# The attention tiles of a pair run from the last to the first, and the values leave PSUM as high and low part

## Chip, cores and metric

The kernel runs on one core of one Trainium2 chip. The metric is the device time of one execution in microseconds; a time is the median of the runs.

## What is computed

One layer of a streaming encoder, for a prompt of 512 frames and a sample of 32 frames with 512 cached ones. Only the part around the change, cut from the reference:

```
qkv = z[..., :3 * D_ATTN].reshape(B, T, 3, N_HEADS_A, HEAD_DIM_A)
q, k, v = qkv[:, :, 0], qkv[:, :, 1], qkv[:, :, 2]
s = einsum('bqhd,bkhd->bhqk', q, k) * (HEAD_DIM_A ** -0.5) + bias
o_a = einsum('bhqk,bkhd->bqhd', softmax(s), v)      # 8 heads x 64; a frame sees its 64-frame chunk
                                                    # and the 8 chunks before it, so all keys up to there
o_b, wkv1 = rwkv7_time_mix(zx, ...)                 # a gated delta rule over the same 8 heads x 64
merged = gates[..., :D_MODEL] * (o_a @ w_out_attn) + gates[..., D_MODEL:] * (o_b @ w_out_rwkv)
```

Before this stand a norm and the combined input projection, behind it the output projection, a residual and a SwiGLU network. All is float32. For the large products each operand is split into a high part that TensorE takes as fp32r and a low part (value minus high part), and three products are summed.

## The kernel before

The five engines run hand-written programs, each in its own order, and meet only at semaphores. The stage that the change touches lies between the input projection and the product with `w_out_attn`, from 347 to 560 us. It mixes two jobs.

The first job is the RWKV recurrence. The prompt is cut into 16 tiles n, four for each of the four head pairs hp, and two tiles a and b are worked on at once in one round of 16 slots. Slots 0 and 1 form the products of a tile (`p_scores`, masked by `v_masks` into XX, CTs and BDs), slot 2 `p_cv`, slots 3 to 12 five levels of a triangular inverse (a step `p_level_p` and a step `p_level_x` in turn, each followed by a small VectorE operation on Pb or XX), slot 13 `p_wu`, slots 14 and 15 `p_out`. There are 8 rounds, so 128 slots g; a head pair has 32 slots p, two rounds.

The second job, attention, is put into the same slots by hand. At the end of slot p each engine runs what is due for the head pair: scores of a tile at the slots `A_S`, the softmax in the slots behind, and the product with the values at the slots `A_PV`. A tile has 128 query frames of both heads e of the pair; prompt tile t has (t + 1) * 128 keys, and tile 4 is the sample with 512 cached keys and 32 own ones. For head e of a tile the order is: `v_scores` (VectorE, adds the bias and takes the maximum, slot S + e), `a_exp` (ScalarE, S + 1 + e), `v_scale` (VectorE: reciprocal and a multiplication in place in `s_sb`, S + 2 + e), `transposes` (TensorE, S + 3 + e), `a_turned_p` (ScalarE copies to `pt_sb`), `values` (TensorE), `a_values` (ScalarE). For the tile with 512 keys the last steps come one slot later. The next tile's `scores` wait for the semaphore `o_ev`, since both use PSUM banks 6 and 7. In `A_PV[0:2]` the sample's own scores are made (`own_scores`, `v_own`), in `A_PV[2]` the cached keys are transposed.

`a_values` copies a tile's values from PSUM into `oaT`, which is the space of the queries, `qk[:, 0:HP]`. In slot 31 of a pair ScalarE copies all 548 columns to `oah` (rounding to fp32r; it lies over the keys, `qk[:, HP:2 * HP]`), and in slot 0 of the next pair VectorE writes `oal`, the difference, over the queries.

GpSimd prepares the next pair's operands in `prelude` (eleven steps over 548 columns, from the start of a pair's first round on, for pairs 1 to 3 in the pair before), and the low parts of weight units, `low(i)`. ScalarE makes their high parts, `high(i)`; that of the first unit of `w_out_attn` is issued inside the slots:

```
                a_attn(g)
                if g == 16 * NR_ - 12:
                    act.wait_ge(sc_mm, NT - TT)
                    act.wait_ge(saved, HP - 1)
                    high(U_OA, U_OA % 2)
```

This is slot 20 of pair 3. `low(U_OA)` waits for it on GpSimd. After the last slot come the sample's recurrence (`p_scores(NT)` and on), the chain of states, and the product with `w_out_attn` (`attn_tile`), which reads `oah` and `oal`.

Of the kernel before, what the change touches and what calls it, by code (L numbers as in the profile page):

```python
# [17 lines left out]
F32 = mybir.dt.float32  # L18
# [32 lines left out]
def build(nc, x_prompt, x_sample, cache_k, cache_v, state_wkv, state_shift, c_prompt, c_sample, w_ada, b_ada,  # L51
# [34 lines left out]
    with ctx:  # L86
# [63 lines left out]
        oaT = qk[:, 0:HP]  # L150
# [192 lines left out]
        A_S = (0, 6, 12, 18, 25)  # L343
        A_PV = (5, 11, 17, 24, 30)

        def head_at(p, after, late=0):

            for t, s in enumerate(A_S):
                for e in range(2):
                    if p == s + after + e + (late if t == 3 else 0):  # L350
                        return t, e
            return None

        def scored(t):

            return TILES[t][1], (t + 1) * P if t < TT else T + TS
# [193 lines left out]
        def _(pool):  # L550
# [85 lines left out]
            link(pool.memset(E1[1][:, 0:1], 1.0))  # L636
            for hp in range(HP):
                if hp:
                    pool.wait_ge(sc_mm, (hp - 1) * TT)
                    pool.wait_ge(gm_dve, (hp - 1) * TT)  # L640
                    for k in range(11):
                        prelude(pool, link, hp, k)
                else:
                    pool.wait_ge(ew_done, 1)
                q = hp % 2
                for x, y in zip(four, (kt[q], bh[q], kh[q], rt[q], bl[q], kl[q])):
                    pool.tensor_copy(x[:, hp, :], y[:, S0:W])
                pool.tensor_copy(four[6][:, hp, :], zs[:, 2 * HP + hp, 1 + S0:1 + W])
                pool.tensor_copy(e4[:, hp:hp + 1], E1[q][:, W:W + 1]).then_inc(saved, 1)
# [13 lines left out]
        def _(act):  # L663
# [187 lines left out]
            def a_exp(hp, t, e):  # L851
                rows_, n = scored(t)
                act.wait_ge(s_biased, 2 * (hp * KS + t) + e + 1)
# [4 lines left out]
            def a_turned_p(hp, t, e):  # L858
                i = hp * KS + t
# [8 lines left out]
            def a_values(hp, t):  # L868
                c0, rows_ = TILES[t]
                act.wait_ge(o_mm, hp * KS + t + 1)  # L870
                act.activation(oaT[:, hp, c0:c0 + rows_], ps[:, 6, 0:rows_], ACT.Copy).then_inc(o_ev, 1)

            def a_attn(u):
# [12 lines left out]
                if p == 31:  # L886
                    act.wait_ge(o_ev, hp * KS + KS)
                    act.activation(oah[:, hp, :], oaT[:, hp, :], ACT.Copy).then_inc(oah_done, 1)
# [110 lines left out]
        def _(dve):  # L999
# [199 lines left out]
            def v_scores(hp, t, e):  # L1199
                rows_, n = scored(t)  # L1200
                i = hp * KS + t
# [21 lines left out]
            def v_scale(hp, t, e):  # L1223
                rows_, n = scored(t)
                i = 2 * (hp * KS + t) + e + 1
# [5 lines left out]

            def v_attn(u):
                hp, p = divmod(u, 32)
                if p == 0 and hp:
                    dve.wait_ge(oah_done, hp)
                    tt(oal[:, hp - 1, :], oaT[:, hp - 1, :], oah[:, hp - 1, :].bitcast(F32), ALU.subtract)  # L1236
                if hp == HP:
                    return
# [25 lines left out]
            v_attn(16 * NR_)  # L1264
# [172 lines left out]
        def _(pe):  # L1437
# [296 lines left out]
            def scores(hp, t):  # L1734
                c0, rows_ = TILES[t]
                i = hp * KS + t
                if i:
                    pe.wait_ge(o_ev, i)
                if t in (1, 2):
                    pe.wait_ge(own_ev, 2 * hp + t)  # L1740
                if t == 3:
# [12 lines left out]
            def transposes(hp, t, e):  # L1754
                rows_ = TILES[t][1]
                pe.wait_ge(p_scaled, 2 * (hp * KS + t) + e + 1)
# [7 lines left out]
            def values(hp, t):  # L1764
# [3 lines left out]
                pe.wait_ge(pt_ev, 2 * (hp * KS + t) + 2)  # L1768
# [74 lines left out]
            def chain(c):  # L1843
# [6 lines left out]
                ins.then_inc(chain_mm, 1)  # L1850
            p_scores(NT)
# [157 lines left out]
```

## Time and profile before

| What | Value |
|---|---|
| median of 3 runs | 1149.13 us (1146.98 to 1151.62) |
| the profiled execution | 1151.87 us, its span 1149.8 us |
| TensorE busy | 1080.1 us, 94% |
| VectorE, ScalarE, GpSimd busy | 400.1, 342.1, 362.5 us |
| TensorE's share of the chain that ended last | 85% |
| mean granted clock of TensorE | 0.967 of full speed |

The busy shares are means over stages of different kind. The rows further down are of the mixing stage only. A timeline row gives the start, the duration, engine, line and operation with the tile written and those read, and in brackets how long the engine had stood idle before and what ended that. PE is TensorE, DVE VectorE, ACT ScalarE, POOL GpSimd.

### The profile page before, as it was taken

The page shows a single profiled execution, that of the slowest core. Times are in us where ns is not written, and L with a number is a line of the kernel's source. Part 1 is how long each engine was busy: PE and PEld are TensorE (multiplying, and loading weights), DVE is VectorE, ACT ScalarE, POOL GpSimd, SP SyncE. Part 2 cuts the span into 40 slices and gives each one's busy share as a digit, 9 for nine tenths or more (in the row PEclk, how much of TensorE's full clock was granted, in tenths as well). Part 3 has the DMA queues.
Part 4 walks back from the last instruction along what each step waited for, and adds up shares of the span by engine and source line. Part 5 has one row for each costly group of instructions (what it writes and reads, how often), then busy time and mean ns, then how long its engine had stood idle before and what let it go on. Part 6 is the DMA issues. An engine that isn't in the chain of part 4 may idle for free.

```text
span 1149.8 us, 25415 instructions
## 1 busy us (share of the span) xinstructions
PE 1080.1 (94%) x11068; PEld 991.9 (86%) x11068; DVE 400.1 (35%) x928; ACT 342.1 (30%) x605; POOL 362.5 (32%) x246
## 2 busy tenths in 40 slices
PE   6799999999998988999897899999999999899995
PEld 5698899999896766777785799999999999899995
DVE  2400100085054666666436746322222222100003
ACT  4521122233333444445121223332232232211112
POOL 0554443333315041301120233334334334243330
PEclk9899999999998999999995999999999999999998
DMA  9865556233201000040250322222422322223211
GB/s 367 296 229 184 183 184 212 96 126 127 85 30 35 21 3 20 12 156 2 85 152 10 123 92 74 74 73 73 109 73 74 109 73 66 72 76 94 82 50 78
DMA packets 115882, 117.31 MB, mean 102 GB/s; under 512 B 5284, under 2 KB 102736, under 8 KB 112472
## 3 DMA queue, kind: packets, MB, share of 16 engines
q1 hardware_dynamic: 111296, 110.74, 30.0%
q10 hardware_dynamic: 4504, 5.36, 1.5%
q8 instruction: 67, 1.10, 0.4%
q14 instruction: 15, 0.12, 0.0%
HBM read 104.59 MB, written 11.49 MB: 101 GB/s over the span
## 4 chain that ended last, share of the span: by engine, by line
PE 85%; DVE 7%; DMA 2%; ACT 2%; issue 1%; SPq 1%; POOL 1%; DVEq 0%; ACTq 0%; POOLq 0%
PE ps L1439 82%; DMA ada_w<-in_w_ada 2%; PE ps L1758 2%; SPq L430 1%; DVE s_sb L1196 1%; POOL w_lo L567 1%; PE ps L1658 1%; DMA gring<-g_d 0%; DVE oal L1236 0%; DVE s_sb L1230 0%; PE ps L1978 0%; DVE Pb L1167 0%; DVE y_sb L1432 0%; DVE ss8b L1335 0%; ACT y_sq L992 0%
## 5 line engine op out<-in xcount | busy, mean ns | idle before, releaser
L567 POOL TENSOR_TENSOR w_lo<-w_raw,w_hi 128x2048 fp32r<-128x2048 f32 (+1 forms) x67 | 287.5, 4290 | 633.7 <-ACT w_hi L697 633.7
L1439 PE MATMUL ps<-hh,w_hi 128*128 128x274 f32 x1376 | 292.1, 294 | 5.0 <-DVE hl L1050 3.5
L1439 PE MATMUL ps<-hh,w_lo 128*128 128x274 f32 x1376 | 290.3, 292 | 0.0
L1439 PE MATMUL ps<-hl,w_hi 128*128 128x274 f32 x1376 | 288.4, 291 | 0.0
L1439 PEld LDWEIGHTS ps<-hh,w_hi 128*128 128x128 f32 x1376 | 220.3, 191 | 11.7 <-issue 9.5
L1439 PEld LDWEIGHTS ps<-hl,w_hi 128*128 128x128 f32 x1376 | 219.8, 191 | 0.0
L1439 PEld LDWEIGHTS ps<-hh,w_lo 128*128 128x128 f32 x1376 | 219.7, 191 | 0.0
L697 ACT ACTIVATE w_hi<-w_raw 128x2048 fp32r<-128x2048 f32 (+1 forms) x67 | 119.3, 1781 | 115.0 <-PE ps L1439 110.6
L1439 PE MATMUL ps<-ah,w_hi 128*128 128x274 f32 x352 | 74.1, 292 | 3.8 <-DVE al L1411 3.8
L1439 PE MATMUL ps<-ah,w_lo 128*128 128x274 f32 x352 | 74.1, 292 | 0.0
L1439 PE MATMUL ps<-al,w_hi 128*128 128x274 f32 x352 | 74.0, 292 | 0.0
L1439 PEld LDWEIGHTS ps<-ah,w_hi 128*128 128x128 f32 x352 | 56.5, 192 | 4.0 <-issue 4.0
L1439 PEld LDWEIGHTS ps<-ah,w_lo 128*128 128x128 f32 x352 | 56.4, 191 | 0.0
L1439 PEld LDWEIGHTS ps<-al,w_hi 128*128 128x128 f32 x352 | 56.4, 191 | 0.0
L1403 DVE TENSOR_TENSOR ff_a<-ps,rstd 128x548 f32<-128x548 f32 x22 | 16.0, 729 | 113.7 <-PE ps L1439 113.6
L978 ACT ACTIVATE ah<-ff_a 128x548 f32 (+1 forms) x22 | 14.6, 664 | 133.8 <-DVE ff_a L1407 133.8
L1370 DVE SCALAR_TENSOR_TENSOR xT<-ps,mod,xT 128x274 f32<-128x274 f32 (+1 forms) x16 | 8.0, 500 | 132.7 <-PE ps L1439 132.7
L1439 PE MATMUL ps<-XX,Pb 64*64 64x64 f32 x672 | 42.5, 230 | 2.6 <-DVE Pb L1167 2.6
L1439 PE MATMUL ps<-Pb,XX 64*64 64x64 f32 x536 | 38.2, 238 | 2.0 <-DVE Pb L1167 2.0
L1439 PEld LDWEIGHTS ps<-XX,ATs 64*64 64x64 f32 x672 | 26.8, 147 | 14.7 <-issue 9.0
L1439 PE MATMUL ps<-XX,ATs 64*64 64x64 f32 x672 | 34.3, 240 | 3.9 <-DVE XX L1177 2.0
L1439 PEld LDWEIGHTS ps<-Pb,XX 64*64 64x64 f32 x536 | 29.0, 146 | 9.4 <-DVE Pb L1167 7.0
(354 smaller groups left out, 1493.9 us busy)
## 6 DMA issues: line engine op xcount, KB each, us to landing
w_raw<-in_w_ffn_in SPq DMA_DIRECT2D x44, 512.0 KB, 4.5
w_raw<-in_w_in SPq DMA_DIRECT2D x42, 512.0 KB, 4.9
ada_l<-in_w_ada SPq DMA_DIRECT2D x16, 1024.0 KB, 6.0
ada_w<-in_w_ada SPq DMA_DIRECT2D x8, 1024.0 KB, 14.2
w_raw<-in_w_ffn_out SPq DMA_DIRECT2D x16, 384.0 KB, 3.9
w_raw<-in_w_ffn_out SPq DMA_DIRECT2D x16, 320.0 KB, 3.2
g_d<-gst SPq DMA_DIRECT2D x16, 274.0 KB, 2.6
gring<-g_d SPq DMA_DIRECT2D x16, 274.0 KB, 4.3
```

The source lines that it names most:

```text
L430: sp.dma_start(ada_w[k][:, :], ada_rows(0, k)).then_inc(ada_in[k], 16)
L567: pool.tensor_tensor(w_lo[:, s, 0:cols], w_raw[:, s, 0:cols], w_hi[:, s, 0:cols].bitcast(F32), ALU.subtract).then_inc(lo_done, 1)
L697: act.activation(w_hi[:, s, 0:cols], w_raw[:, s, 0:cols], ACT.Copy).then_inc(hi_done, 1)
L978: act.activation(ah[:, i - U_UP, :], ff_a[:, :], ACT.Copy).then_inc(ah_done, 1)
L1196: return dve.tensor_tensor_reduce(out=out, in0=x, in1=y, scale=-1.0, scalar=first, op0=ALU.add, op1=ALU.min, accum_out=low)
L1370: link(stt(xa[:, 0:H], ps[:, 2 * q, 0:H], g(0), xa[:, 0:H], ALU.mult, ALU.add))
L1403: tt(halves(ff_a[:, :]), pair(1), halves(rstd2[:, :]), ALU.mult).then_inc(pair_free, 1)
L1439: return pe.matmul(out, lhsT, rhs, start=start, stop=stop)
L1658: ins = pe.transpose(bank(q, 2)[:, i * P:(i + 1) * P], x, ident[:, :])
L1758: ins = pe.transpose(ps[:, 6 + e, b * rows_:(b + 1) * rows_], s_sb[0:rows_, e, b * P:(b + 1) * P], ident[0:rows_, 0:rows_])
```

## The change

The prompt tiles of a pair are taken in the order 3, 2, 1, 0, then the sample (`A_TILE`), and the slots are spaced anew: the tile with 512 keys has slots 0 to 6. The helpers are now called with the place i in this order, and look up the tile t. Since a key tile is no longer needed once the query tile of the same frames is done, `a_values` writes the fp32r high part of a tile straight from PSUM over its keys, and the new `v_values` on VectorE writes the low part, PSUM minus high part, over its queries; `o_ev` is now raised by VectorE. `oaT`, the whole-pair copy in slot 31 and the whole-pair subtraction in the next slot 0 are gone. GpSimd zeroes the four padding columns of both parts once, and TensorE waits for the last `o_ev` ahead of `p_scores(NT)`.

```diff
--- before.py
+++ after.py
@@ -147,7 +147,6 @@
         kc_raw, vcs = at("kc_raw", [P, TT, P], RAW + 2560), at("vcs", [P, TT, P], RAW + 4608)
         pt_sb, s_sb, rsum = at("pt_sb", [P, 2, T + P], HL + 7168), at("s_sb", [P, 2, T + TS], LO + 2560), \
             at("rsum", [P, 2, 4], LO + 6912)
-        oaT = qk[:, 0:HP]
         oah, oal = at("oah", [P, HP, W], E + 8768, F32R), at("oal", [P, HP, W], E, F32R)
 
 
@@ -340,19 +339,21 @@
             return [x[:, c] for x in (kt[q], bh[q], kh[q], rt[q], bl[q], kl[q])] + [zs[:, 2 * HP + hp, 1 + t * P:1 + (t + 1) * P]]
 
 
-        A_S = (0, 6, 12, 18, 25)
-        A_PV = (5, 11, 17, 24, 30)
+        A_S = (0, 7, 13, 19, 25)
+        A_PV = (6, 12, 18, 24, 30)
+        A_TILE = list(range(TT - 1, -1, -1)) + [TT]
 
         def head_at(p, after, late=0):
 
-            for t, s in enumerate(A_S):
+            for i, s in enumerate(A_S):
                 for e in range(2):
-                    if p == s + after + e + (late if t == 3 else 0):
-                        return t, e
+                    if p == s + after + e + (late if i == 0 else 0):
+                        return i, e
             return None
 
-        def scored(t):
-
+        def scored(i):
+
+            t = A_TILE[i]
             return TILES[t][1], (t + 1) * P if t < TT else T + TS
 
         def prelude(eng, link, hp, k):
@@ -634,6 +635,8 @@
                 low(i, i % 2)
             pool.wait_ge(unit_mm, U_OA)
             link(pool.memset(E1[1][:, 0:1], 1.0))
+            for x in (oah, oal):
+                link(pool.memset(x[:, :, T:S0].bitcast(F32), 0.0))
             for hp in range(HP):
                 if hp:
                     pool.wait_ge(sc_mm, (hp - 1) * TT)
@@ -848,15 +851,15 @@
                     i = act.activation(NN[:, hp, 2 * t + c, :], b[:, L:2 * L], ACT.Copy)
                 i.then_inc(gm_act, 1)
 
-            def a_exp(hp, t, e):
-                rows_, n = scored(t)
-                act.wait_ge(s_biased, 2 * (hp * KS + t) + e + 1)
+            def a_exp(hp, i, e):
+                rows_, n = scored(i)
+                act.wait_ge(s_biased, 2 * (hp * KS + i) + e + 1)
                 v = s_sb[0:rows_, e, 0:n]
                 act.activation(v, v, ACT.Exp, bias=rsum[0:rows_, e, 1:2], scale=-1.0, accum_out=rsum[0:rows_, e, 0:1])\
                    .then_inc(p_done, 1)
 
-            def a_turned_p(hp, t, e):
-                i = hp * KS + t
+            def a_turned_p(hp, i, e):
+                t, i = A_TILE[i], hp * KS + i
                 n = (t + 1) * P if t < TT else TT * TS
                 act.wait_ge(pt_mm, 2 * i + e + 1)
                 if i and e == 0:
@@ -865,10 +868,10 @@
                     act.activation(pt_sb[0:TS, e, n:n + TS], ps[0:TS, 6 + e, n:n + TS], ACT.Copy)
                 act.activation(pt_sb[:, e, 0:n], ps[:, 6 + e, 0:n], ACT.Copy).then_inc(pt_ev, 1)
 
-            def a_values(hp, t):
-                c0, rows_ = TILES[t]
-                act.wait_ge(o_mm, hp * KS + t + 1)
-                act.activation(oaT[:, hp, c0:c0 + rows_], ps[:, 6, 0:rows_], ACT.Copy).then_inc(o_ev, 1)
+            def a_values(hp, i):
+                c0, rows_ = TILES[A_TILE[i]]
+                act.wait_ge(o_mm, hp * KS + i + 1)
+                act.activation(oah[:, hp, c0:c0 + rows_], ps[:, 6, 0:rows_], ACT.Copy).then_inc(oah_done, 1)
 
             def a_attn(u):
                 hp, p = divmod(u, 32)
@@ -883,9 +886,6 @@
                 if p == A_PV[2]:
                     act.wait_ge(kct_mm, hp + 1)
                     act.activation(kcT[:, :], ps[:, 7, :], ACT.Copy).then_inc(kct_ev, 1)
-                if p == 31:
-                    act.wait_ge(o_ev, hp * KS + KS)
-                    act.activation(oah[:, hp, :], oaT[:, hp, :], ACT.Copy).then_inc(oah_done, 1)
 
             for g in range(16 * NR_):
                 rnd, p = divmod(g, 16)
@@ -1196,9 +1196,9 @@
                 return dve.tensor_tensor_reduce(out=out, in0=x, in1=y, scale=-1.0, scalar=first, op0=ALU.add, op1=ALU.min,
                                                 accum_out=low)
 
-            def v_scores(hp, t, e):
-                rows_, n = scored(t)
-                i = hp * KS + t
+            def v_scores(hp, i, e):
+                rows_, n = scored(i)
+                t, i = A_TILE[i], hp * KS + i
                 dve.wait_ge(s_mm, i + 1)
                 if i:
                     dve.wait_ge(pt_mm, 2 * i - 1 + e)
@@ -1220,22 +1220,25 @@
                 low_of(s_sb[0:TS, e, T:T + TS], ps[0:TS, 7, e * TS:(e + 1) * TS],
                        bias[0:TS, hp * 2 + e, T - P:T - P + TS], HUGE, rsum[0:TS, e, 3:4]).then_inc(own_ev, 1)
 
-            def v_scale(hp, t, e):
-                rows_, n = scored(t)
-                i = 2 * (hp * KS + t) + e + 1
+            def v_scale(hp, i, e):
+                rows_, n = scored(i)
+                i = 2 * (hp * KS + i) + e + 1
                 dve.wait_ge(p_done, i)
                 dve.reciprocal(rsum[0:rows_, e, 2:3], rsum[0:rows_, e, 0:1]).then_inc(rs_inv, 1)
                 dve.wait_ge(rs_inv, i)
                 v = s_sb[0:rows_, e, 0:n]
                 sts(v, v, rsum[0:rows_, e, 2:3], None, ALU.mult).then_inc(p_scaled, 1)
 
+            def v_values(hp, i):
+                c0, rows_ = TILES[A_TILE[i]]
+                c = slice(c0, c0 + rows_)
+                dve.wait_ge(oah_done, hp * KS + i + 1)
+                tt(oal[:, hp, c], ps[:, 6, 0:rows_], oah[:, hp, c].bitcast(F32), ALU.subtract).then_inc(o_ev, 1)
+
             def v_attn(u):
                 hp, p = divmod(u, 32)
-                if p == 0 and hp:
-                    dve.wait_ge(oah_done, hp)
-                    tt(oal[:, hp - 1, :], oaT[:, hp - 1, :], oah[:, hp - 1, :].bitcast(F32), ALU.subtract)
-                if hp == HP:
-                    return
+                if p in A_PV:
+                    v_values(hp, A_PV.index(p))
                 if head_at(p, 2, 1):
                     v_scale(hp, *head_at(p, 2, 1))
                 if head_at(p, 0):
@@ -1261,7 +1264,6 @@
                 if p == 9 and rnd % 2 and rnd < NR_ - 1:
                     v_bonus(rnd // 2 + 1)
                 v_attn(g)
-            v_attn(16 * NR_)
 
 
             dve.wait_ge(gm_act, NT)
@@ -1731,14 +1733,14 @@
                 p_chunks(q, part, (bank(q, 0)[:, L:2 * L], bank(q, 2)[:, L:2 * L]),
                          (bank(q, 1)[:, L:2 * L], bank(q, 2)[:, 3 * L:4 * L])).then_inc(gm_mm, 1)
 
-            def scores(hp, t):
+            def scores(hp, i):
+                t = A_TILE[i]
                 c0, rows_ = TILES[t]
-                i = hp * KS + t
-                if i:
-                    pe.wait_ge(o_ev, i)
-                if t in (1, 2):
-                    pe.wait_ge(own_ev, 2 * hp + t)
-                if t == 3:
+                if hp or i:
+                    pe.wait_ge(o_ev, hp * KS + i)
+                if i in (1, 2):
+                    pe.wait_ge(own_ev, 2 * hp + i)
+                if i == 3:
                     pe.wait_ge(kct_ev, hp + 1)
                 for e in range(2):
                     q_ = qk[part[e], hp, c0:c0 + rows_]
@@ -1751,9 +1753,10 @@
             def own_scores(hp, e):
                 mm(ps[0:TS, 7, e * TS:(e + 1) * TS], qk[part[e], hp, S0:W], qk[part[e], HP + hp, S0:W]).then_inc(own_mm, 1)
 
-            def transposes(hp, t, e):
+            def transposes(hp, i, e):
+                t = A_TILE[i]
                 rows_ = TILES[t][1]
-                pe.wait_ge(p_scaled, 2 * (hp * KS + t) + e + 1)
+                pe.wait_ge(p_scaled, 2 * (hp * KS + i) + e + 1)
                 for b in range(min(t + 1, TT)):
                     ins = pe.transpose(ps[:, 6 + e, b * rows_:(b + 1) * rows_], s_sb[0:rows_, e, b * P:(b + 1) * P],
                                        ident[0:rows_, 0:rows_])
@@ -1761,11 +1764,12 @@
                     ins = pe.transpose(ps[0:TS, 6 + e, TT * TS:(TT + 1) * TS], s_sb[0:TS, e, T:T + TS], ident[0:TS, 0:TS])
                 ins.then_inc(pt_mm, 1)
 
-            def values(hp, t):
+            def values(hp, i):
+                t = A_TILE[i]
                 rows_ = TILES[t][1]
                 c = [slice(hp * P + e * DH, hp * P + (e + 1) * DH) for e in range(2)]
                 o = [ps[part[e], 6, 0:rows_] for e in range(2)]
-                pe.wait_ge(pt_ev, 2 * (hp * KS + t) + 2)
+                pe.wait_ge(pt_ev, 2 * (hp * KS + i) + 2)
                 if t == TT:
                     pe.wait_ge(vc_in, hp * 16 + 16)
                 for b in range(min(t + 1, TT)):
@@ -1848,6 +1852,7 @@
                                  MT[part[e], a, c, :] if c < NCH else MT4[part[e], a, :],
                                  SS[part[e], c if c < NCH else NCH + 1, a, :])
                 ins.then_inc(chain_mm, 1)
+            pe.wait_ge(o_ev, HP * KS)
             p_scores(NT)
             pe.wait_ge(gm_dve, NT)
             pe.wait_ge(gm_act, NT)
```

## Rows read from the trace of the kernel before

**Rows 1.** Windows: pairs 0 and 1, and the sum over the stage.

```profile
core 0: us, PE busy (x) PEld busy (x) DVE busy (x) ACT busy (x) POOL busy (x), PEclk, DMA share, GB/s
347.20:399.60 52.40, 47.68 (x1006) 37.35 (x1010) 29.98 (x120) 22.37 (x73) 16.43 (x28) 0.90 0.09 26
399.60:449.70 50.10, 43.95 (x1018) 34.70 (x1011) 33.09 (x123) 22.24 (x77) 15.76 (x23) 0.97 0.05 14
...
sum 212.80, PE 189.09 PEld 149.75 DVE 132.79 ACT 92.11 POOL 53.83; mean PE 37.82 PEld 29.95 DVE 26.56 ACT 18.42 POOL 10.77
```

**Rows 2.** Waits of TensorE from 347 to 560 us.

```profile
engine line waited for: us in total, times, longest us
PE ps L1439 <- DVE BDs L1159: 9.5, 5, 3.1
PE ps L1439 <- DVE Pb L1167: 4.6, 11, 0.6
```

**Rows 3.** Timeline of VectorE, start of pair 1.

```profile
402.00 1.32 DVE L1162 TENSOR_TENSOR XX<-XX,dg 128x256 f32<-128x256 f32 x1
403.24 1.86 DVE L1236 TENSOR_TENSOR oal<-qk,oah 128x548 fp32r<-128x548 f32 x1
405.02 0.28 DVE L1196 CUSTOM_DVE_ANT_0 s_sb<-ps,bias 128x128 f32<-128x128 f32 x1
...
405.23 0.41 DVE L1156 TENSOR_TENSOR XX<-ps,nM 128x256 f32<-128x256 f32 x1
...
405.77 0.41 DVE L1159 TENSOR_TENSOR BDs<-ps,inclU 128x256 f32<-128x256 f32 x1
```

**Rows 4.** Timeline of GpSimd, start of pair 1.

```profile
401.67 1.37 POOL L374 TENSOR_TENSOR kh<-kh,zs 128x548 f32<-128x548 f32 x1
```

**Rows 5.** Timeline of TensorE: the waits at four places.

```profile
353.35 1.12 PE L1439 MATMUL ps<-XX,ATs 64*64 64x64 f32 x16 [1.49 <-ACT KC L834]
...
406.23 0.45 PE L1439 MATMUL ps<-tk,CTs 64*64 64x64 f32 x8 [3.13 <-DVE BDs L1159]
...
424.76 0.55 PE L1758 MATMUL ps<-ident,s_sb 128*128 128x128 f32 x3 [0.69 <-DVE s_sb L1230]
...
504.67 0.45 PE L1439 MATMUL ps<-tk,CTs 64*64 64x64 f32 x8 [1.09 <-DVE BDs L1159]
```

**Rows 6.** Timeline of TensorE: scores of 128 and 512 columns, one level step.

```profile
400.90 0.49 PE L1439 MATMUL ps<-qk 64*128 64x128 f32 x4
...
430.46 1.13 PE L1439 MATMUL ps<-qk 64*128 64x512 f32 x4 [0.17 <-ACT kcT L885]
431.52 0.68 PE L1439 MATMUL ps<-XX,ATs 64*64 64x64 f32 x16
```

**Rows 7.** Windows of TensorE alone, start of pair 2.

```profile
core 0: us, PE busy (x), PEclk, DMA share, GB/s
...
456.00:462.00 6.00, 5.67 (x76) 0.50 0.00 0
```

**Rows 8.** Groups by form on VectorE, and line L871 on ScalarE.

```profile
L1196 DVE CUSTOM_DVE_ANT_0 s_sb<-ps,bias 128x512 f32<-128x512 f32 x8 | 5.5, 687 | 7.5 <-PE ps L1439 7.5
...
L871 ACT ACTIVATE qk<-ps x20: 204/278/280, 358.9 to 546.4; 128x128 f32<-128x128 f32 x16, 128x32 f32<-128x32 f32 x4
```

**Rows 9.** Timelines of ScalarE, GpSimd and VectorE, pair 3, slots 20 to 22.

```profile
531.42 0.72 ACT L855 ACTIVATE s_sb<-s_sb,rsum 128x512 f32<-128x512 f32 x1 [0.19 <-DVE rsum L1196]
...
532.14 1.90 ACT L697 ACTIVATE w_hi<-w_raw 128x2048 fp32r<-128x2048 f32 x1
...
534.27 4.74 POOL L567 TENSOR_TENSOR w_lo<-w_raw,w_hi 128x2048 fp32r<-128x2048 f32 x1 [63.58 <-ACT w_hi L697]
...
534.15 0.48 DVE L1230 TENSOR_SCALAR s_sb<-s_sb,rsum 128x512 f32<-128x512 f32 x1
```

**Rows 10.** Line L1117 on VectorE.

```profile
engine op xcount: duration ns min/median/max, first and last start us, forms
L1117 DVE TENSOR_SCALAR kk<-zs,par x4: 491/493/4744, 263.5 to 269.0; 128x548 f32<-128x548 f32 x4
```

**Rows 11.** Timelines of VectorE and GpSimd, pair 1, slots 8 and 9.

```profile
415.82 0.79 DVE L1230 TENSOR_SCALAR s_sb<-s_sb,rsum 128x256 f32<-128x256 f32 x1
...
415.11 1.34 POOL L395 TENSOR_TENSOR kh<-kh,E 128x548 f32<-128x548 f32 x1
```

**Rows 12.** Timelines of VectorE and TensorE after the last slot.

```profile
548.75 0.73 DVE L1236 TENSOR_TENSOR oal<-qk,oah 128x548 fp32r<-128x548 f32 x1 [0.95 <-ACT oah L888]
...
549.74 0.68 PE L1439 MATMUL ps<-SS,MT 64*64 64x64 f32 x16 [0.74 <-DVE SS L1268]
```

## The prediction

> **What bounds the kernel.** I read the busy shares first (TensorE is busy 94% of the span), then the chain that ended last (85% TensorE), so only what makes TensorE wait or run slowly can move the end. All edits lie in the 128 slots of the mixing stage. The windows [rows 1] show TensorE at work for 47.7 of 52.4 us in pair 0, for 43.95 of 50.1 in pair 1, and for 189.1 of 212.8 in the stage, so it is idle some 24 us. The table of waits [rows 2] puts 9.5 of these on the masked products (BDs) and 4.6 on Pb. No edit here can give back more than that and its clock effects.
>
> The largest wait stands at the start of a pair [rows 3]: VectorE masks tile a, then takes 1.86 us for the low part of the pair before (oal), then masks tile b, and TensorE stands 3.13 us until BDs of tile b is there [rows 5]. Both VectorE operations are long because GpSimd holds something they need: its tensor operation runs from 401.67 to 403.04 [rows 4], and the addition to XX that starts at 402.00 ends 0.3 us after that [rows 3]. In the last pair GpSimd is idle and the same wait is 1.09 us. After its wait TensorE runs a while at half clock [rows 7].
>
> **Removed.** Four whole-pair oal operations on VectorE (slot 0 of the next pair, and one after the last slot) and four whole-pair oah copies on ScalarE. Between masks(a) and masks(b) 1.86 us of VectorE goes away in pairs 1 and 2.
>
> **Put in the same place.** The last tile is now the first in a pair, so scores of 512 columns stand in slot 0: TensorE 1.13 us for 0.49 [rows 6], +0.64, which is only moved work (it leaves slot 18), and VectorE 0.69 for 0.28 [rows 3, 8], +0.41, between masks(a) and masks(b). Pairs 1 and 2: masks(a) ends at about 403.3, scores to 404.0, BDs(b) 0.95 us later (405.23 to 406.18 in [rows 3]) at 404.9. TensorE has 0.64 more to do and is free at 403.75 instead of 403.1; it waits about 1.2 us for 3.13: -1.9 each. But the scale of these 512 columns by 1/sum (0.48 us free, [rows 9]) now falls in slots 3 and 4, where GpSimd begins a run of operations as long as that in [rows 4]; each of the two heads can be held up to one operation. I take 0.8 exposed per pair (between 0 and 2.7), so -1.1 each. Pair 3, GpSimd idle: 1.09 becomes about 0.3, -0.8. Pair 0 had no oal, so it only gets the longer work: ScalarE's exponential of 512 columns (0.72, [rows 9]) for one of 128 stands ahead of the KC copies for which TensorE waits 1.49 us [rows 5]: +0.5. Sum of the starts: -2.5 us (bounds -6 and +1).
>
> **The new hand-over.** Each of 20 tiles: ScalarE writes oah from PSUM (0.28, the operation it had, [rows 8]) and VectorE adds a subtraction from PSUM, 0.28 for 128 columns by the equally wide operation in [rows 3], 20 times 5.3 us in all against 5.2 removed. It reads PSUM and one SBUF tile, as the mask operation does that starts at 405.23. VectorE waits in its queue for the values (at the end of slot PV) and for ScalarE; behind it stand the slot's own scores and the next slot's Pb or XX. It is held about 0.65 us after the values' last product. TensorE meanwhile has the next slot's level step (0.6 to 1.0 us, [rows 6]) and waits for o_ev only behind that, and the scores then cover VectorE's lag: nothing for most. Where VectorE is already late I charge 0.2 us twice per pair (slots 8 to 10, and 25 where the sample's scores are due): +1.6 in four pairs. Without that cover each costs 0.65.
>
> **The middle of a pair.** The tile at slots 13 to 18 has 256 columns instead of 384, and its transposes move one slot later. The 0.69 us wait at 424.76 [rows 5] goes; but nothing then stands between p_out and the next p_scores, which must wait for both evacuations (about 0.4 to 0.5), and the second scale now stands behind masks(c) (0.2, and 0.2 again at masks(d)). I count +0.35 there and -0.38 where the first tile's two 0.69 us operations no longer delay Pb in slot 19: zero, give or take 0.3 per pair.
>
> **The end.** VectorE's chain of states waited for oah and for oal (0.73 us), and TensorE 0.74 us for it [rows 12]. Both are gone from there: -0.8. The new wait for o_ev ahead of the sample's p_scores was met a slot and a half earlier. Two small memsets on GpSimd come ahead of preparations that then wait for ScalarE anyway: nothing, at most 0.3 us.
>
> **The step that costs.** In pair 3 ScalarE issues high(U_OA) (1.90 us) at the end of slot 20, and GpSimd's subtraction of 2,048 columns follows 0.23 us after its end, for 4.74 us [rows 9]. Before, both exponentials of the tile in slot 18 came ahead of high, and the second scale began at 534.15, 0.12 us ahead of GpSimd. Now the tile starts in slot 19: its second exponential is in slot 21, behind high in ScalarE's queue. So the second scale, which needs it, cannot start before about 0.5 us (exponential and reciprocal, estimate) after GpSimd has begun. What a tensor_scalar with SBUF alone does then is seen from 263 us on, under the same subtraction of another unit: at least one of L1117's four takes 4.74 us, where the median is 0.49 [rows 10]. So VectorE stands for about 4 us; TensorE has one level step left, then waits for this scale to transpose: from about 4.85 us after slot 19's start to 8.8 us: +3.9. The first scale I place 0.4 us ahead of GpSimd; if it fails too, the stall is about 1 us longer. Bounds of the term: 0 and 5.5.
>
> The nearest rows for a scale itself are milder: a 256-column scale that starts at 415.82, inside GpSimd's operation of 1.34 us, takes 0.79 us and is done 0.16 us after that operation's end [rows 11]. Read as "held till GpSimd is done" this also gives the 4 us; read as "up to 0.4 us longer" it gives no stall and a sum 6 us lower, rival (a) below. I take the first, because the end of the scale follows GpSimd's end and because of L1117.
>
> The Trainium skill, page SBUF — State Buffer, section "Who interferes with whom", speaks against this change: the two engines share a port pair under an exclusive lock, tensor_scalar can enter the modes that take it, and whichever issues second "fully blocks" for the other's whole instruction. By that rule the stall is there in full; this case's rows agree (0.79 us at 415.82, 4.74 at L1117).
>
> **Clock.** In pair 2, after the wait at its start, TensorE worked at a granted clock of 0.50, the 1.2 GHz level, from 456 to 462 us [rows 7]; half of those 5.7 us of work is lost, 2.8 us. The mean of pair 1, 0.97 of 50 us [rows 1], gives 3 us at that level and 1.5 lost. The new stall of 3.9 us is longer than either wait: +2.2, the middle of the two. The shorter waits at the starts of pairs 1 to 3 may spare some of what those lose now, 2.8 and twice 1.5 to 2, so 6 us; I count a third, -1.9 (between 0 and -6).
>
> **Sum.** Starts -2.5, hand-over +1.6, middle 0, end -0.8, stall +3.9, clock +0.3: +2.5 us. On the profiled execution (1151.87 us, span 1149.8) that gives 1154.4. That run is 2.7 us above the median of 1149.13, so the median forecast is 1151.6 us, +0.2%. A measurement of this kernel can tell about 0.5% (5.7 us) from no change.
>
> **Rivals.**
> (a) No stall in pair 3: the scale escapes GpSimd, or narrow scales are not held. For: the one at 534.15 escaped by 0.12 us, and the row of L1117 is of an operation four times as wide. Against: ScalarE's order, which puts the exponential behind high, and the 0.79 us of [rows 11]. Then -3.9 and -2.2: 1145.5 us; with all of the clock loss at the starts spared too, 1141.4.
> (b) The hand-over is not covered: VectorE's wait for TensorE and ScalarE, 20 times. For: its idle time in the level slots is mostly waiting for TensorE, so a late start is passed on. Against: TensorE waits for Pb only 11 times in the stage's 128 slots [rows 2], so its own work mostly covers VectorE's lag. Half of 0.65 us exposed, 20 times, adds 6.5 less the 1.6 counted: 1156.5. It decides from about 0.25 us per tile.
> (c) The half clock after the stall lasts as in pair 0, where a mean of 0.90 over 52 us [rows 1] means about 10 us so: 2.8 us more, 1154.4.
> (d) The starts gain more than the port takes: the scales of slots 3 and 4 slip between GpSimd's operations: -1.6, and the clock is spared, -4: 1146.
>
> **Chances.** Forecast 0.55, (a) 0.16, (b) 0.12, (c) 0.08, (d) 0.09. Faster by over 0.5% (under 1143.4) needs (a) with spared clocks: 0.09. Slower (over 1154.9) is most of (b) and part of (c): 0.15. Within 0.5%: 0.76. The range of 8 in 10 is 1143.5 to 1156.5: below, (a) with part of the clock; above, (b).
>
> **What would show it.** Right: oal operations of 0.28 us; the start waits at 1.2, 1.2 and 0.3; one tensor_scalar of s_sb, 128 by 128, of about 4 us near 534 us, and TensorE waiting some 3.9 us for it; oah gone from 548 us. Wrong: that scale at 0.29 us; BDs waits still near 3; waits for Pb or o_ev grown in the slots after values.

## The result, and the profile after

The changed kernel takes 1153.01 us (median of 5 runs, 1152.42 to 1154.43); the kernel before, beside it, 1148.16 (5 runs, 1146.98 to 1151.62). The ratio is 1.0035 (95% interval 1.0019 to 1.005): slower, by less than the 0.5% that I called measurable, though the interval is clear of 1, and 1.4 us above the forecast of 1151.6. The profiled execution took 1152.97 us, its span is 1151.2, so it stands at its median, as that of before did not.

Windows of the changed kernel by pair and behind the last, columns as in [rows 1]:

```profile
core 0: us, PE busy (x) PEld busy (x) DVE busy (x) ACT busy (x) POOL busy (x), PEclk, DMA share, GB/s
348.00:400.50 52.50, 46.54 (x1006) 36.37 (x1010) 31.64 (x125) 22.59 (x73) 17.11 (x31) 0.93 0.10 26
400.50:448.40 47.90, 43.08 (x1018) 33.71 (x1012) 32.41 (x128) 22.11 (x76) 16.18 (x23) 1.00 0.05 14
448.40:496.30 47.90, 43.10 (x1019) 33.71 (x1013) 32.38 (x127) 22.10 (x76) 16.17 (x23) 1.00 0.05 14
496.30:547.10 50.80, 43.42 (x1014) 33.96 (x1007) 33.63 (x125) 22.58 (x75) 4.50 (x1) 0.97 0.24 89
547.10:561.10 14.00, 11.02 (x249) 9.90 (x245) 7.00 (x22) 1.89 (x8) 1.17 (x2) 0.76 0.49 153
```

The last three stretches of the kernel before, whose first two are in [rows 1]:

```profile
449.70:500.10 50.40, 44.83 (x1018) 35.53 (x1013) 32.70 (x123) 22.24 (x77) 15.74 (x23) 0.93 0.05 13
500.10:546.80 46.70, 43.02 (x1011) 34.04 (x1006) 29.49 (x121) 22.94 (x76) 4.74 (x1) 0.96 0.26 97
546.80:559.80 13.00, 9.41 (x260) 7.92 (x249) 7.44 (x23) 2.33 (x9) 1.17 (x2) 1.00 0.55 163
```

Length less PE busy is TensorE's idle time. Before it was 4.7, 6.2, 5.6, 3.7 and 3.6 us in these five stretches, 23.7 in all; now it is 6.0, 4.8, 4.8, 7.4 and 3.0, 25.9. Busy time fell from 188.9 to 187.2: 2.6 us less in pairs 1 and 2, which now run at full clock, 1.1 less in pair 0, and 2.0 more in pair 3 and behind it. Waits of TensorE, the scales of before first and then those of the changed kernel, which answer [rows 2]:

```profile
PE ps L1758 <- DVE s_sb L1230: 3.3, 5, 0.8
...
PE ps L1761 <- DVE s_sb L1230: 8.0, 10, 3.6
PE ps L1441 <- DVE BDs L1159: 5.3, 5, 1.8
PE ps L1441 <- DVE Pb L1167: 3.6, 9, 0.6
PE ps L1441 <- DVE MT L1189: 2.4, 4, 0.7
PE ps L1441 <- ACT KC L837: 2.2, 2, 1.8
```

BDs gave back 4.2 us; the scales of `s_sb` took 4.7, of which 3.6 is one wait; MT, which VectorE writes from the products of `p_out`, is new. KC is a tile that ScalarE copies from PSUM ahead of the first level step. The start of pair 1, VectorE, GpSimd and TensorE, answers [rows 3 to 5]:

```profile
402.90 1.31 DVE L1162 TENSOR_TENSOR XX<-XX,dg 128x256 f32<-128x256 f32 x1
...
407.54 1.31 DVE L1230 TENSOR_SCALAR s_sb<-s_sb,rsum 128x512 f32<-128x512 f32 x1
...
409.35 1.07 DVE L1230 TENSOR_SCALAR s_sb<-s_sb,rsum 128x512 f32<-128x512 f32 x1
...
407.20 1.36 POOL L380 TENSOR_TENSOR kt<-kk,E 128x548 f32<-128x548 f32 x1 [1.78 <-ACT E L774]
...
408.99 1.16 POOL L384 TENSOR_TENSOR rt<-zs,E 128x548 f32<-128x548 f32 x1
...
405.74 0.45 PE L1441 MATMUL ps<-tk,CTs 64*64 64x64 f32 x8 [1.09 <-DVE BDs L1159]
408.91 0.66 PE L1761 MATMUL ps<-ident,s_sb 128*128 128x128 f32 x4 [0.62 <-DVE s_sb L1230]
410.48 0.66 PE L1761 MATMUL ps<-ident,s_sb 128*128 128x128 f32 x4 [0.31 <-DVE s_sb L1230]
```

The whole-pair low part is gone from between the masks, and the wait for BDs is 1.09 us for 3.13. Each 512-column scale that needed 0.48 us in [rows 9] now ends a little after the GpSimd operation it met, and TensorE pays 0.93 for the two. In pair 3, ScalarE, GpSimd, VectorE and TensorE:

```profile
527.33 0.40 ACT L858 ACTIVATE s_sb<-s_sb,rsum 128x128 f32<-128x128 f32 x1 [1.01 <-DVE rsum L1196]
...
527.73 1.89 ACT L700 ACTIVATE w_hi<-w_raw 128x2048 fp32r<-128x2048 f32 x1
529.53 0.39 ACT L858 ACTIVATE s_sb<-s_sb,rsum 128x128 f32<-128x128 f32 x1
...
529.86 4.50 POOL L568 TENSOR_TENSOR w_lo<-w_raw,w_hi 128x2048 fp32r<-128x2048 f32 x1 [61.70 <-ACT w_hi L700]
...
529.32 0.29 DVE L1230 TENSOR_SCALAR s_sb<-s_sb,rsum 128x128 f32<-128x128 f32 x1
...
530.43 4.00 DVE L1230 TENSOR_SCALAR s_sb<-s_sb,rsum 128x128 f32<-128x128 f32 x1
...
534.49 0.33 PE L1761 MATMUL ps<-ident,s_sb 128*128 128x128 f32 x1 [3.63 <-DVE s_sb L1230]
```

The second exponential stands behind `high(U_OA)`, its scale starts 0.57 us after GpSimd's subtraction and ends 0.07 after it. Where the clock was low, TensorE alone:

```profile
core 0: us, PE busy (x), PEclk, DMA share, GB/s
354.00:361.00 7.00, 5.89 (x72) 0.52 0.01 2
410.00:417.00 7.00, 6.53 (x128) 1.00 0.01 4
458.00:465.00 7.00, 6.40 (x124) 1.00 0.01 2
534.00:539.00 5.00, 4.51 (x57) 0.66 0.00 0
552.00:559.00 7.00, 6.22 (x110) 0.52 0.54 176
```

A PEclk of 1.00 is full speed, 0.50 half clock. The stretches of half clock behind the starts of pairs 1 to 3 are gone (behind that of pair 3, too, PEclk is 1.00 from 502 to 510 us); there are two new ones, behind the stall and after the last slot.

### The profile page after: what moved, and what is told of

It reads as the page before. It is cut to its first block, busy times and chain, and to the rows that moved or that the text cites. A ratio compares the mean times of both kernels' runs of the same rounds, so it can differ in the third digit from the quotient of the medians.

```text
span 1151.2 us, 25429 instructions
## 1 busy us (share of the span) xinstructions
PE 1078.3 (94%) x11068; PEld 989.5 (86%) x11068; DVE 403.9 (35%) x944; ACT 340.9 (30%) x601; POOL 363.4 (32%) x248
## 4 chain that ended last, share of the span: by engine, by line
PE 84%; DVE 7%; DMA 2%; ACT 2%; issue 2%; SPq 1%; POOL 1%; DVEq 0%; ACTq 0%; POOLq 0%
PE ps L1441 81%; DMA ada_w<-in_w_ada 2%; PE ps L1761 1%; DVE s_sb L1230 1%; SPq L431 1%; DVE s_sb L1196 1%; POOL w_lo L568 1%; PE ps L1660 1%; DMA gring<-g_d 0%; PE ps L1983 0%; DVE y_sb L1434 0%; DVE XX L1177 0%; DVE ss8b L1337 0%; DVE XX L1156 0%; DVE Pb L1167 0%
## 5 line engine op out<-in xcount | busy, mean ns | idle before, releaser
L1403 DVE TENSOR_TENSOR ff_g<-ps,rstd 128x548 f32<-128x548 f32 x22 | 16.0, 729 | 58.9 <-PE ps L1441 58.9
```

Of the source, the lines that this page charges most:

```text
L1403: tt(halves(ff_g[:, :]), pair(0), halves(rstd2[:, :]), ALU.mult).then_inc(pair_free, 1)
```

## The experiments

They ask three things: what the stall in pair 3 costs, what the new order and the new value path cost each, and how much VectorE loses to GpSimd elsewhere. Their expectations say "port" for what VectorE and GpSimd were thought to share. Times of before given beside a run are of the same chip.

**Both kernels again.** e0_before_again is the kernel before, e10_change_again the changed one, unedited.

> The kernel before, unchanged: a second profile and the width of the comparison. The first profiled execution took 1151.87 us against a median of 1148.2. If that difference is TensorE's clock, this profile is shorter by 2 to 4 us with fewer or shorter stretches at half clock and the same waits; if the waits themselves vary, they differ between the two profiles. Ratio to before within 0.3% of 1.

1149.90 us, ratio 1.0005 (0.9991 to 1.0018). TensorE's waits were those of [rows 2] to 0.1 us, but pair 0 took 49.7 us for 52.4:

```profile
348.00:397.70 49.70, 44.99 (x1005) 35.31 (x1008) 29.81 (x120) 22.30 (x73) 16.39 (x28) 0.97 0.10 27
```

So executions of one program differ in how long TensorE stays at half clock, not in what it waits for. The execution profiled first had lost 2.7 us more in pair 0 than this one (busy 47.7 against 45.0). e2_before_high_slot19, further down, runs the same program up to slot 19 of pair 3, and its pair 0 ran at full clock: 48.5 us, busy 43.6.

> The change itself once more, on the same chip as these. Theory: 1.0035 times the kernel before again within its interval, 1152 to 1154; the same 4.0 us scale and 3.6 us wait, with half clock behind it. If the wait is the same and the half clock lies elsewhere, the clock is what differs between executions.

1152.83 us (12 runs; 1149.81 before), ratio 1.0021 (1.0004 to 1.0038); the 3.63 us wait and both new stretches of half clock stood where they had been.

**The stall.** e1_high_slot21 moves ScalarE's high part one slot on, behind the second exponential; e2_before_high_slot19 makes the same race in the kernel before; e5_low_held leaves the high part in slot 20 and holds GpSimd instead.

```diff
 e1_high_slot21 (on the changed kernel)
-                if g == 16 * NR_ - 12:
+                if g == 16 * NR_ - 11:
 e2_before_high_slot19 (on the kernel before)
-                if g == 16 * NR_ - 12:
+                if g == 16 * NR_ - 13:
 e5_low_held (on the changed kernel, GpSimd)
+            pool.wait_ge(p_scaled, 2 * (3 * KS + 3) + 2)
             low(U_OA, U_OA % 2)
```

> The changed kernel, only ScalarE's high part of the first w_out_attn unit is issued at the end of slot 21 of pair 3 instead of slot 20, so behind both exponentials of the tile. Port theory: the second scale (128x128) takes 0.29 us instead of 4.00, TensorE's 3.63 us wait at 534 us is gone and with it the half clock behind it (about 2 us lost), so 5 to 6 us less than the change's 1153.0: about 1147.5, level with the kernel before. Rival (the 20 hand-overs on VectorE cost the time, the wait at 534 is made good later): no more than 1 us less, about 1152.5.

1145.97 us (1149.22 before), ratio 0.9967 (0.9952 to 0.9982): faster. Its windows, pair 3 and the rest; the first three pairs are as in the changed kernel to 0.1 us:

```profile
496.50:542.30 45.80, 41.96 (x1014) 32.99 (x1007) 29.82 (x125) 22.58 (x75) 4.52 (x1) 1.00 0.27 99
542.30:555.20 12.90, 9.13 (x248) 7.82 (x244) 7.02 (x22) 1.89 (x8) 1.16 (x2) 1.00 0.52 164
```

Pair 3 is 5.0 us shorter, 3.5 of it idle time and 1.5 clock; the rest is 1.1 shorter, 1.9 less of busy time and 0.8 more of idle time. One slot in ScalarE's queue was worth 7.0 us by the medians (6.3 to 8.1, each less its own before), where 5 to 6 was expected.

> The kernel before with nothing but high moved one slot earlier (19), so ahead of the second exponential of its 512-column tile. Port theory: the second scale of that tile is held by GpSimd's subtraction, about 4 us instead of 0.48, TensorE waits 3 to 4 us, and the time rises by 4 to 6 us to 1152 to 1154. Rival (the stall comes from the new tile order or from the hand-over): the scale stays at 0.48 us and the time at 1148 to 1149.

1158.09 us, ratio 1.0074 (1.0048 to 1.0099). The stall came where it was expected, in its VectorE and TensorE timelines:

```profile
530.05 4.05 DVE L1230 TENSOR_SCALAR s_sb<-s_sb,rsum 128x512 f32<-128x512 f32 x1
...
534.16 1.11 PE L1758 MATMUL ps<-ident,s_sb 128*128 128x128 f32 x4 [3.36 <-DVE s_sb L1230]
```

A scale four times as wide takes the same 4 us. The median rose by 8.9 us where 4 to 6 was expected. Its profile shows half clock (mean 0.57) from 532 to 540 us and 0.72 from 552 to 558, but its span was only 4.6 above that of e0_before_again. That is the execution whose pair 0 ran at full clock, 1.2 us shorter than in e0_before_again and 3.9 shorter than in the first profile; whether the others, up to 7.4 us longer, lost more there isn't shown.

> The changed kernel, high again in slot 20, but GpSimd's subtraction of that unit waits until the tile's second scale is done. It tells the port from ScalarE's order. Port theory: the second scale takes 0.29 us though its exponential still comes behind high; TensorE waits at most 0.3 us there; 1146 to 1147.5. Rival (the exponential that high delays by 1.9 us is itself the stall): TensorE still waits 2 us or more and the time is 1150 or more.

1145.41 us, ratio 0.9954 (0.9937 to 0.9971). The high part is still ahead of the exponential; VectorE and GpSimd:

```profile
529.82 0.29 DVE L1231 TENSOR_SCALAR s_sb<-s_sb,rsum 128x128 f32<-128x128 f32 x1
...
530.33 4.51 POOL L568 TENSOR_TENSOR w_lo<-w_raw,w_hi 128x2048 fp32r<-128x2048 f32 x1 [62.80 <-DVE s_sb L1231]
```

Same time as e1_high_slot21: what cost the 4 us is GpSimd being ahead of the scale, not ScalarE's 1.89 us in front of the exponential.

**Order and value path.** e3_order_alone keeps the new order and slots, but takes the values through `oaT`, with the whole-pair high part in slot 31 and the whole-pair low part in the next slot 0, as before. e6_order_high_slot21 is the same with the high part in slot 21.

```diff
 e3_order_alone, e6_order_high_slot21
-                act.activation(oah[:, hp, c0:c0 + rows_], ps[:, 6, 0:rows_], ACT.Copy).then_inc(oah_done, 1)
+                act.activation(oaT[:, hp, c0:c0 + rows_], ps[:, 6, 0:rows_], ACT.Copy).then_inc(o_ev, 1)
...
+                if p == 31:
+                    act.wait_ge(o_ev, hp * KS + KS)
+                    act.activation(oah[:, hp, :], oaT[:, hp, :], ACT.Copy).then_inc(oah_done, 1)
...
-                if p in A_PV:
-                    v_values(hp, A_PV.index(p))
+                if p == 0 and hp:
+                    dve.wait_ge(oah_done, hp)
+                    tt(oal[:, hp - 1, :], oaT[:, hp - 1, :], oah[:, hp - 1, :].bitcast(F32), ALU.subtract)
```

> The new tile order and slots, with the old way of the values (float32 copy, whole-pair high part in slot 31, whole-pair low part in the next slot 0). Theory: the 4 us scale is there as in the changed kernel, the waits for BDs at the pair starts come back at 3 us or more in pairs 1 and 2, the end is 0.7 us longer: 1156 to 1159. Rival (hand-over costs): without 20 subtractions and their waits VectorE is early, and it is faster than the change, 1150 or less.

1157.78 us, ratio 1.0066 (1.0048 to 1.0085), with BDs waits of 8.7 us (longest 2.9) and a wait of 3.6 for the scale.

> Tile order alone (old way of the values) with high in slot 21. Against the first experiment (1146.0) it gives the worth of the hand-over without the stall. Theory: the whole-pair low parts cost 1.9 us on VectorE at the starts of pairs 1 and 2, 0.7 at that of pair 3 and at the end, and half clock follows: 4 to 5 us more, 1150 to 1151, and no faster than the kernel before. Rival (the hand-over on VectorE costs about what it spares): 1146 to 1147.

1150.98 us (1149.9 before), ratio 1.0005 (0.9994 to 1.0016). Against e1_high_slot21 the stage is 211.9 us for 207.0: the value path by tiles gains about 5 us in the stage (4.3 in the medians, each less its own before). Only 1.1 of these are idle time. The other 3.8 are clock: 3.2 in pairs 1 and 2, whose BDs waits were long again (8.7 us in the stage for 5.4), and 2.1 in the stretch after the last slot, less 1.5 that pairs 0 and 3 had better. The order with its slots is worth nothing, or up to 1 us of loss. e3 less e6 is the stall again: 6.8 us (7.5, each less its own before).

**Is the hand-over covered?** e8_values_twice is e1_high_slot21 with every low part computed twice.

```diff
+                link(tt(oal[:, hp, c], ps[:, 6, 0:rows_], oah[:, hp, c].bitcast(F32), ALU.subtract))
                 tt(oal[:, hp, c], ps[:, 6, 0:rows_], oah[:, hp, c].bitcast(F32), ALU.subtract).then_inc(o_ev, 1)
```

> The changed kernel with high in slot 21, and the low part of every tile computed twice on VectorE, each hand-over some 0.35 us longer (20 times, 7 us of VectorE's time). Theory (TensorE's level steps and scores cover the hand-over): under 1.5 us more than 1146.0. Rival (the hand-over is exposed): 4 to 7 us more, 1150 to 1153.

1148.79 us (1149.9 before), ratio 0.9985 (0.9971 to 0.9998), some 2.1 us above e1_high_slot21 by medians and 2.8 by the stage, for 7.6 us more busy time of VectorE (408.0 for 400.4): 5.4 are the added subtractions, and 2.1 are scales of `s_sb` that ran longer (22.4 for 20.3), among them the two of 512 columns in pair 0, 1.23 and 1.26 us for 0.79 and 0.62. The time is between the two expectations. So a third or so of what was put in is exposed, and some of that comes by way of the scales (TensorE's waits for them rose from 4.3 to 4.8 us): the cover is there and thin. New waits of TensorE stand for it: 1.7 us for oal (4 times) and 1.6 for rsum (3).

**GpSimd out of the way.** e4_prelude_held is e1_high_slot21 with GpSimd's preparations of the next pair held until the first tile of this one has been transposed.

```diff
                 if hp:
...
+                    pool.wait_ge(pt_mm, 2 * (hp - 1) * KS + 2)
                     for k in range(11):
                         prelude(pool, link, hp, k)
```

> The changed kernel with high in slot 21 (as in the first experiment, 1146.0), and GpSimd's preparations for the next pair held until the transposes of the pair's first tile are done, so that they meet neither the masks nor the first tile's scales. Port theory: at the starts of pairs 1 and 2 the addition to XX takes 0.42 us instead of 1.31, the 512-column scales 0.49 instead of 1.31 and 1.07, the waits for BDs fall from 1.09 to about 0.3 and those for the scales (0.62, 0.31) go: 3 us less, 1143. Rival (the held preparations collide with later scales, in slots 9, 10 and 15, 16): those waits grow by as much, 1146.

1143.39 us (1149.9 before), ratio 0.9931 (0.9916 to 0.9947). The same VectorE operations of pair 1 with GpSimd away, and the windows of pairs 0 and 1:

```profile
400.16 0.42 DVE L1163 TENSOR_TENSOR XX<-XX,dg 128x256 f32<-128x256 f32 x1
...
404.51 0.49 DVE L1231 TENSOR_SCALAR s_sb<-s_sb,rsum 128x512 f32<-128x512 f32 x1
...
405.82 0.49 DVE L1231 TENSOR_SCALAR s_sb<-s_sb,rsum 128x512 f32<-128x512 f32 x1
```

```profile
346.80:397.80 51.00, 45.46 (x1009) 35.47 (x1013) 30.32 (x125) 22.61 (x73) 16.74 (x30) 0.97 0.10 26
397.80:444.70 46.90, 42.86 (x1014) 33.55 (x1010) 30.95 (x127) 21.89 (x76) 15.75 (x23) 1.00 0.05 14
```

Each of pairs 1 and 2 is 1.0 us shorter and pair 0 1.5, of which 1.1 is clock. The wait for BDs in pair 1 fell to 0.7 us, not to the 0.3 expected, with 0.4 for KC behind it, and waits for the scales remain (2.3 us in the stage for 4.3). The end lost 1.4 of it again, to a stretch at half clock from 544 to 551 us.

**The old slots.** Does the stall hang on slot 19? e7_old_slots is the changed kernel with the old slot lists; e9_old_slots_held adds the hold of e4_prelude_held, e11_old_slots_both that and the hold of e5_low_held.

```diff
-        A_S = (0, 7, 13, 19, 25)
-        A_PV = (6, 12, 18, 24, 30)
+        A_S = (0, 6, 12, 18, 25)
+        A_PV = (5, 11, 17, 24, 30)
...
-                    if p == s + after + e + (late if i == 0 else 0):
+                    if p == s + after + e + (late if i == 3 else 0):
```

> The changed kernel (tile order 3, 2, 1, 0, hand-over from PSUM) on the old slots: scores at 0, 6, 12, 18, 25, values at 5, 11, 17, 24, 30, the extra slot again with the tile at 18, high in slot 20 as before. Both exponentials of the last prompt tile (slots 19, 20) come ahead of high again. Theory (it is the slots, not the order of the tiles, that let GpSimd in): no scale above 1.4 us, no wait of 3.6 us, 1145 to 1147. Rival (any version of the new order meets GpSimd's subtraction): a scale of about 4 us and 1152 or more.

1151.17 us (1149.81 before), ratio 1.0003 (0.9987 to 1.0019): a miss, the stall was there. ScalarE, GpSimd and VectorE:

```profile
525.46 0.40 ACT L858 ACTIVATE s_sb<-s_sb,rsum 128x128 f32<-128x128 f32 x1 [0.33 <-DVE rsum L1196]
...
525.87 1.90 ACT L700 ACTIVATE w_hi<-w_raw 128x2048 fp32r<-128x2048 f32 x1
...
527.99 4.50 POOL L568 TENSOR_TENSOR w_lo<-w_raw,w_hi 128x2048 fp32r<-128x2048 f32 x1 [63.15 <-ACT w_hi L700]
...
528.55 4.03 DVE L1230 TENSOR_SCALAR s_sb<-s_sb,rsum 128x128 f32<-128x128 f32 x1
```

Both exponentials are ahead of the high part, as in [rows 9], but they are of 128 columns: 0.40 us for 0.72. Counted back from the second scale, the second exponential starts 0.36 us earlier than before (3.09 us ahead of it for 2.73), as the scores that VectorE makes for it are shorter too, and it is 0.32 shorter. So the high part starts 0.68 us earlier against the scale, GpSimd follows it, and it is there 0.56 us before the scale, where before the scale was 0.12 us ahead.

> The same, with GpSimd's preparations held until the transposes of the pair's first tile are done. Theory: as with the new slots, 2.5 to 3 us less than without the hold, so 1142 to 1144. Rival (with one slot less for the 512-column tile the collisions come back in slots 8 and 9): 1145 or more.

1152.24 us, ratio 1.0017 (1.0002 to 1.0033): a miss too, with the same wait of 3.65 us. Its pairs 1 and 2 were 47.0 us in the profile, whose execution took 1148.28, among the shortest of its 12; why most took 4 us more isn't shown (in the profile pair 0 ran at full clock).

> The changed kernel with the old slot list, the prelude held back in each pair, and GpSimd's low part of the first output unit held back until the second scale of the tile at slot 18 has been done. Port theory (the 3.65 us wait of the two runs with the old slots is the same GpSimd subtraction catching the scale, now because the tile at slot 18 is 128 columns wide and its exponentials are shorter, so that GpSimd starts earlier): no scale of 128 by 128 over 1.4 us in pair 3, no wait of TensorE over 1 us there, span 1141 to 1144 us, median 1143 to 1147 us. Rival (the old slots stall for a reason of their own, such as the order of ScalarE's copies): the wait of 3.65 us near 529 us stays, and the time is that of the run before it, about 1152 us.

1142.77 us (6 runs, 1139.38 to 1145.88; 1149.1 before), ratio 0.9948 (0.9928 to 0.9968), just under the 1143 to 1147 expected. Its two holds keep both scales of the tile at 0.29 us:

```profile
526.26 0.29 DVE L1232 TENSOR_SCALAR s_sb<-s_sb,rsum 128x128 f32<-128x128 f32 x1
...
526.77 4.51 POOL L568 TENSOR_TENSOR w_lo<-w_raw,w_hi 128x2048 fp32r<-128x2048 f32 x1 [56.12 <-DVE s_sb L1232]
```

That settles the two misses: with the old slots too the stall is GpSimd ahead of the scale. Against e9_old_slots_held, which differs by that one hold, it is 8.8 us faster, each less its own before. This version, e5_low_held and e4_prelude_held are the best here, 0.5 to 0.7% under the kernel before; their intervals overlap.

## Why the prediction was right, and where it was off

The forecast can be checked by pair, in idle time of TensorE (my terms without the clock; hand-over and middle spread over the pairs) against the differences of the windows:

| | forecast | measured |
|---|---|---|
| pair 0 | +0.9 | +1.2 |
| pair 1, pair 2 | -0.7 each | -1.3, -0.8 |
| pair 3 | +3.5 | +3.7 |
| after the last slot | -0.8 | -0.6 |
| idle in all | +2.2 | +2.2 |
| busy (clock) | +0.3 | -1.7, or +1.0 against e0_before_again |

**The starts.** Right for pairs 1 and 2: 1.09 us where I had 1.2, and 0.93 for the held scales where I had 0.8. In pair 0 the wait for KC rose from 1.49 to 1.77, less than the 0.5 charged. Wrong for pair 3, where I had 0.3:

```profile
501.06 0.45 PE L1441 MATMUL ps<-tk,CTs 64*64 64x64 f32 x8 [0.67 <-DVE BDs L1159]
501.89 0.68 PE L1441 MATMUL ps<-XX,ATs 64*64 64x64 f32 x16 [0.38 <-ACT KC L837]
```

It is 0.67 for BDs and 0.38 more for KC, 1.05 together, so the 0.8 was not gained. I had followed VectorE only; ScalarE's copies of KC were next.

**The hand-over.** The 20 low parts, by their line:

```profile
L1236 DVE TENSOR_TENSOR oal<-ps,oah x20: 191/291/292, 363.7 to 546.8; 128x128 fp32r<-128x128 f32 x16, 128x32 fp32r<-128x32 f32 x4
...
  ACT oah L874: 15.7, 20
...
  PEld ps L1441: 1.3, 6
```

VectorE stands 15.7 us in front of them, 0.8 each where I had 0.65, and TensorE's loads waited 1.3 us for them, 1.6 forecast. Waits for Pb and XX, by which a late VectorE would show too, are 5.7 us for 6.6 before. Rival (b), half of each exposed, is ruled out by these rows and by an idle time that rose by 2.2 in all, as forecast.

**The middle.** The wait for MT ahead of the next `p_scores` is 0.57 to 0.68 us in all four pairs, in place of the 0.69 that went: about zero, as forecast.

**The step that costs.** Right in mechanism and size: the exponential behind the high part, GpSimd 0.57 us ahead (0.5 forecast), a 128-column scale of 4.00 us, TensorE waiting 3.63 (3.9). e1_high_slot21 and e5_low_held show it from both sides, ScalarE's order and GpSimd's start; their 1145.97 and 1145.41 us are what rival (a) gave for no stall, 1145.5. The reading of [rows 11] as "held till GpSimd is done" is borne out at 4.00, 4.05, 1.31 and 1.07 us, each of which ended within 0.3 us of the GpSimd operation it met. Rival (d), that the scales slip between these, is ruled out by the same rows.

The Trainium skill, page SBUF — State Buffer, section "Who interferes with whom", says of a VectorE instruction in a two-port mode and a GpSimd instruction that whoever issues second is blocked for the other's whole instruction; the trace agrees, with 4.00 us against 0.29 and an end 0.07 us after GpSimd's. The same section counts a VectorE instruction with two SBUF inputs among those that contend with a GpSimd instruction that reads SBUF, and one with at most one SBUF input and no two-port mode not. The trace agrees: the addition to XX took 1.31 us and 0.42 with GpSimd held back, and the low part from PSUM never more than 0.292, also at 413.60 us, 0.13 after the start of a GpSimd operation of 1.34.

**The end.** Idle time fell by 0.6 (0.8 forecast): the waits of 0.74 and 1.46 us became one of 1.80. In the changed kernel a stretch at half clock ate it.

**The clock** is the term that was mis-sized, twice. Behind the starts of pairs 1 to 3 all of the loss went, 3.7 us in busy time between before and e1_high_slot21 (131.8 to 128.1). I had put the whole loss at 6 and counted a third, 1.9. The stall took 1.5 in pair 3. The half-clock stretch after the last slot took 1.9 more; it went with the stall in e1_high_slot21 and e5_low_held, but e4_prelude_held and e6_order_high_slot21 have one without a stall, so that it belongs to the stall is not shown. With it the loss is 3.4 where I had 2.2. The two errors nearly cancel, which is luck, and rival (c), 5.0 us of clock for the stall, was not reached.

A third term I left at nothing is pair 0. Its busy time is 46.5 us in the changed kernel, 1.1 less than in the profile that I started from and 1.5 more than in e0_before_again, which stands at its median. I carried a difference from an execution 2.7 us above its median over to the median. Against the second profile of before, the change costs 1.9 us idle and 1.0 busy, and its span is 3.2 us longer. That may account for the 1.4 us that are missing, but the base itself moves by as much: the change is 4.9 us above 1148.16 in the first comparison and 3.0 above 1149.81 in e10_change_again.

**In sum** the change is one gain and one loss: about -4 to -5 us for the value path, and +6 to +8 for a stall that one slot number removes. The order costs nothing, or up to 1 us.

## What to carry to other kernels

When an order written out by hand is changed, look for long GpSimd operations and for what now starts just behind them on VectorE: a margin of 0.12 us decided on 3.6 us of wait and 1.5 to 3.4 of clock, and with the old slots exponentials that got 0.3 us shorter and started 0.4 earlier were enough to lose it. Guard such a pair by a semaphore on the scale, as in e5_low_held, not by a slot. And profile the kernel before twice, since one execution can carry some 3 us of half clock that the median doesn't.

## What the runs showed that I had not expected

- The half-clock stretches follow small changes: pair 0 ran at a mean clock of 0.90 and 0.97 in two executions of one program with equal waits, at 0.93 in the changed kernel, and at full clock (347 to 370 us) with the old slots. The last need not be the slots' doing: in e2_before_high_slot19 the program of before ran pair 0 at full clock too.
- The stretch after the last slot appears with the stall (552 to 559 us, 0.52) and goes with it in e1_high_slot21 (1.00 from 547 to 554), but also appears without any stall in e4_prelude_held (0.57 from 544 to 551) and in e6_order_high_slot21 (0.57 from 549 to 556). What sets it off stays open.
- A held scale's time goes by how much of GpSimd's operation is left, not by the scale's width: 4.00 us for 128 columns, begun with 3.93 left, and 4.05 for 512, begun with 3.77 left.
